# GLA stage of a hybrid layer on one core: from whole-sequence passes in fp32 to eight units of head pair and quarter with split fp32r products

## What is computed

```
gq, gk, gv, glr, gg = split(h @ w_in[:, :GLA_IN])         # 256, 256, 512, 16, 512 columns
log_a = log_sigmoid(glr @ gla_gate_up + gla_gate_bias) / 16
q = gq * 64**-0.5                                         # 4 heads, dk 64, dv 128
# chunks of 64 tokens, b = cumsum(log_a) within a chunk
q_in, k_in, k_st = q * exp(b), k * exp(-b), k * exp(b_last - b)
scores = tril(q_in @ k_in.T);  o_intra = scores @ v
S = S * exp(b_last) + k_st.T @ v                          # chunk after chunk
o = o_intra + q_in @ S_prev
gla_out = o * rsqrt(mean(o*o) + 1e-6) * gla_norm_w * silu(gg)
```

## Time and profile before

| | us |
|---|---|
| median of 3 runs | 3938.05 (3936.14 to 3941.47) |
| the profiled execution, its own time | 3943.03 |
| its span in the profile | 3941.3 |
| mean granted TensorE clock, share of full speed | 0.954 |
| TensorE busy in the span | 3507.1 |
| VectorE, ScalarE, GpSimd busy | 1894.0, 1273.3, 798.4 |

### The profile page before, as it was taken

One profiled execution on the slowest core, in us unless ns is written; L12 is line 12 of the kernel. 1 busy time (PEld: TensorE's weight loads), 2 busy tenths in 40 slices (PEclk: granted clock), 3 DMA queues, 4 the chain that ended last, 5 costly groups with the idle time before them and its releaser, 6 DMA issues. The chain is left out here.

```text
span 3941.3 us, 72212 instructions
## 1 busy us (share of the span) xinstructions
PE 3507.1 (89%) x30237; PEld 2860.4 (73%) x30237; DVE 1894.0 (48%) x2915; ACT 1273.3 (32%) x1970; POOL 798.4 (20%) x592
## 2 busy tenths in 40 slices
PE   6989989899698898797999998960699999999998
PEld 4777878778534344586888886850699999999997
DVE  4455656556522133366212225669455555555553
ACT  3343534444221222233000002330344444444442
POOL 3333434333167093000000000011010010110100
PEclk9999999999899899898999999985899999999999
DMA  4121121111132131343110105440466666666663
GB/s 129 45 79 45 43 82 43 55 47 29 60 121 79 44 107 33 128 136 94 27 53 27 53 11 183 155 138 13 158 199 218 203 214 204 201 218 207 208 207 86
DMA packets 357752, 431.44 MB, mean 109 GB/s; under 512 B 14788, under 2 KB 301684, under 8 KB 356004
## 3 DMA queue, kind: packets, MB, share of 16 engines
q1 hardware_dynamic: 348328, 394.82, 31.1%
q0 software_dynamic: 9216, 33.56, 3.6%
HBM read 361.04 MB, written 67.13 MB: 109 GB/s over the span
## 5 line engine op out<-in xcount | busy, mean ns | idle before, releaser
L1983 PE MATMUL bank<-ex_x_hi,ex_w_lo 128*128 128x256 f32 x2048 | 580.3, 283 | 1.5 <-DVE ex_x_lo L2152 1.5
L1984 PE MATMUL bank<-ex_x_lo,ex_w_hi 128*128 128x256 f32 x2048 | 580.2, 283 | 0.0
L1985 PE MATMUL bank<-ex_x_hi,ex_w_hi 128*128 128x256 f32 x2048 | 580.1, 283 | 0.0
L1979 DVE TENSOR_TENSOR ex_w_lo<-ex_w_loaded,ex_w_hi 128x2048 fp32r<-128x2048 f32 x186 | 420.7, 2290 | 235.6 <-ACT ex_w_hi L1975 235.6
L1975 ACT ACTIVATE ex_w_hi<-ex_w_loaded 128x2048 fp32r<-128x2048 f32 x192 | 359.8, 1905 | 199.6 <-PE bank L1985 183.9
L1983 PEld LDWEIGHTS bank<-ex_x_hi,ex_w_lo 128*128 128x128 f32 x2048 | 393.9, 192 | 2.5 <-issue 1.9
L1984 PEld LDWEIGHTS bank<-ex_x_lo,ex_w_hi 128*128 128x128 f32 x2048 | 393.8, 192 | 0.6
L1985 PEld LDWEIGHTS bank<-ex_x_hi,ex_w_hi 128*128 128x128 f32 x2048 | 393.8, 192 | 0.0
L1227 PE MATMUL bank<-hidden_hT,gl_w_block 128*128 128x512 f32 x768 | 335.1, 599 | 1.4 <-ACT gl_ada_acc L1341 1.4
L1778 PE MATMUL bank<-sc_x_hi,sc_w_lo 128*128 128x512 f32 x768 | 300.4, 391 | 21.8 <-DVE sc_hT_lo L1814 16.3
L1779 PE MATMUL bank<-sc_hT_lo,sc_w_hi 128*128 128x512 f32 x768 | 299.5, 390 | 0.0
(11 more groups left out here) (334 smaller groups left out, 7083.6 us busy)
## 6 DMA issues: line engine op xcount, KB each, us to landing
ex_w_loaded<-in_wg SPq DMA_DIRECT2D x64, 1024.0 KB, 5.2
ex_w_loaded<-in_wu SPq DMA_DIRECT2D x64, 1024.0 KB, 6.5
ex_w_loaded<-in_wd SPq DMA_DIRECT2D x64, 1024.0 KB, 5.2
rw_w_loaded<-in_w_in SPq DMA_DIRECT2D x68, 512.0 KB, 3.9
gl_ada_tile<-in_ada_w SPq DMA_DIRECT2D x48, 512.0 KB, 3.9
sc_w_loaded<-in_sc_w_in SPq DMA_DIRECT2D x24, 512.0 KB, 6.9
rw_x_tile<-in_x SPq DMA_DIRECT2D x16, 512.0 KB, 4.9
hT_dram<-rw_h_staged SPq DMA_DIRECT2D x32, 256.0 KB, 2.8
```

The costliest lines, as they stand in the source:

```text
L1979: engine.tensor_tensor(w_lo[c % SPLIT][:], raw[:, c % LOADED, :], w_hi[c % SPLIT][:].bitcast(F32), ALU.subtract).then_inc(s["lo"], 1)
L1983: nc.tensor.matmul(psum, ll, rh, start=first, stop=False)
L1984: nc.tensor.matmul(psum, lh, rl, start=False, stop=False)
L1985: return nc.tensor.matmul(psum, lh, rh, start=False, stop=last)
```

## The change

The stage no longer holds h for the whole sequence. It works in eight units u = 4*gp + q, gp a pair of heads and q a quarter of 512 tokens, unrolled, with no barrier in between; `hT` is made after the stage.

- Products: each h quarter is loaded in two halves into one buffer `hs`, split by ScalarE in four pieces of 128 x 1024 (`split_h`) into `h_hi`, and by VectorE (`low_h`) into `h_lo`; one buffer each. The first two pieces of the next quarter may be written when g1 is half done (`h_free`), the others when it is done. The weights of a pair are split once (`split_w`, `low_w`) and stay for its four units. All products are three fp32r matmuls: gate rank (only for u < 4), k, q, g0, g1 with 512 columns; the values token-major (h is the stationary side) with 256 columns, so v needs no turn.
- Two PSUM banks take all jobs in turn (`begin` waits until the job two before has been read).
- Core of unit c = u - 1 among the products of unit u: four turns of k_st, eight score products, 16 state terms in four quadrants, o inside (channel-major: v as the stationary side), o of the state (64 rows, 64 columns, 16 of them), and the variance by a matmul with a matrix of 1/128. A state buffer of 16 chunks lets the eight updates of a unit run one after the other.
- rsqrt and silu come from Exp and Ln: factor = exp(-0.5*ln(var + eps) + log_sigmoid(g)) * g * norm weight; Silu and Sqrt are gone.
- ada: the loads go out six tiles per unit; the same two GpSimd instructions per tile; the six sums of a half in units 3 and 7.
- Stores of 128 x 512 per unit and head.

```diff
-def gla(nc, k, hT, w_in, gate_up, gate_bias_col, norm_col, mT, ada_w, ada_b):
+def gla(nc, k, w_in, gate_up, gate_bias_col, norm_col, mT, ada_w, ada_b):
...
+                def begin(key):
+                    n = len(job)
+                    job[key] = n
+                    before.append(key)
+                    if n >= 2:
+                        pe.wait_ge(*read_of(before[n - 2]))
+                    return bank[RB[n % 2]]
...
+                    for kb in range(KD):
+                        if first:
+                            h_ready(u, kb)
+                        nc.tensor.matmul(psum[0:rows, :], lo[:, kb, :], h_hi[:, kb, :], start=(kb == 0), stop=False)
+                        nc.tensor.matmul(psum[0:rows, :], hi[:, kb, :], h_lo[:, kb, :], start=False, stop=False)
+                        mm = nc.tensor.matmul(psum[0:rows, :], hi[:, kb, :], h_hi[:, kb, :], start=False, stop=(kb == KD - 1))
+                        if last and kb == KD // 2 - 1:
+                            mm.then_inc(s["h_free"], 1)
...
+                for u in range(NU):
+                    c = u - 1
+                    if u < Q:
+                        lr(u)
+                    values(u, 0)
+                    z(u)
+                    if c >= 0:
+                        turn_and_score(c)
+                    values(u, 1)
+                    if c >= 0:
+                        state_terms(c)
+                        o_inside(c)
+                    block_product(u, "k")
+                    if c >= 0:
+                        o_of_state(c)
+                    block_product(u, "q")
+                    if c >= 0:
+                        variance(c)
+                    if u == Q - 1:
+                        ada_sums(u)
+                    block_product(u, "g0")
+                    block_product(u, "g1", True)
+                c = NU - 1
+                turn_and_score(c)
+                state_terms(c)
+                o_inside(c)
+                ada_sums(c)
+                o_of_state(c)
+                variance(c)
...
+                for u in range(NU):
+                    if u + 1 < NU:
+                        load_h(u + 1, 0)
+                        load_h(u + 1, 1)
+                    if u == Q - 1:
+                        load_w(NB)
+                        load_w(NB + 1)
...
+                    for m in range(6 * u, 6 * u + 6):
+                        ada(m)
...
+                    if u:
+                        store(u - 1)
...
+                def keep_gate(u, h):
+                    n = 2 * u + h
+                    psum = psum_of(f"g{h}", u)
+                    act.wait_ge(s["job"], job[(f"g{h}", u)] + 1)
+                    if u:
+                        act.wait_ge(s["mult"], n - 1)
+                    nc.scalar.activation(gn[h][:], psum, ACT.Copy, scale=nw[:, 0:1]).then_inc(s["g_copied"], 1)
+                    nc.scalar.activation(lsg[h][:], psum, ACT.Abs).then_inc(s["g_abs"], 1)
+                    act.wait_ge(s["g_abs"], n + 1)
+                    nc.scalar.activation(lsg[h][:], lsg[h][:], ACT.Exp, scale=-1.0).then_inc(s["g_exp"], 1)
+                    act.wait_ge(s["g_exp"], n + 1)
+                    nc.scalar.activation(lsg[h][:], lsg[h][:], ACT.Ln, bias=1.0).then_inc(s["g_ln"], 1)
...
+                    keep_values(u, 0)
+                    gate(u)
...
+                    if c >= 0:
+                        keep_turned(c)
...
+                    exponents(u)
...
+                    if c >= 0:
+                        square_o(c)
...
+                    if u == Q - 1:
+                        keep_ada(u)
+                    if c >= 0:
+                        log_of_variance(c)
+                        factor(c)
+                    if u == Q - 1:
+                        split_w(NB + 3)
+                    keep_gate(u, 0)
+                    if u + 1 < NU:
+                        for p in range(4):
+                            split_h(u + 1, p)
+                    keep_gate(u, 1)
...
+                    if c >= 0:
+                        combine(c)
...
+                    log_sigmoid(u, 0)
+                    if u + 1 < NU:
+                        for p in range(4):
+                            low_h(u + 1, p)
+                    log_sigmoid(u, 1)
```

More of the change, by code:

```diff
@@ L1147, in gla @@
+        vt = sb(nc, ctx, "v_tokens", [P, 2, 4, 2 * P])
+        ktok = sb(nc, ctx, "k_tokens", [P, 4, P])
+        scm = sb(nc, ctx, "scores", [P, 2, 4, P])
+        S = sb(nc, ctx, "state", [P, 16, P])
+        gn, lsg, osq, fac, ob = [[sb(nc, ctx, f"{n}{h}", [P, QT]) for h in range(2)] for n in ("gate", "log_sigmoid", "o_square", "factor", "out")]
+        mean = sb(nc, ctx, "mean", [P, P])
+        eps = sb(nc, ctx, "eps", [P, 1])
         ada_t = sb(nc, ctx, "ada_tile", [P, 2, ADA_W])
         ada_acc = sb(nc, ctx, "ada_acc", [P, 3 * D])
-        ada_in = (s["ada_w0"], s["ada_w1"])
+        bank = k.bank
@@ L1150, in gla @@
+        heads2 = [slice(0, 64), slice(64, 128)]
+        quads = [(0, 0), (1, 1), (0, 1), (1, 0)]
+        RB = (0, 1)
         NA = 3 * KD
[L1151 to L1156, removed]
-        with nc.Block() as block:
+        blocks = ("v0", "v1", "k", "q", "g0", "g1")
@@ L1159, in _, with load_h @@
             @block.sync
             def _(sp):
-                sp.dma_start(wl[:], wv[:, :, GLA_LR:GLA_LR + RANK]).then_inc(s["wl"], 16)
[L1162 to L1174, removed]
+                def load_h(u, half):
+                    q = u % Q
+                    if u:
+                        sp.wait_ge(s["h_lo"], 4 * u - 2 + 2 * half)
+                    sp.dma_start(hs[:, 4 * half:4 * half + 4, :], k.hT_dram[4 * half:4 * half + 4, :, q * QT:(q + 1) * QT].rearrange("k p t -> p k t")).then_inc(h_in[half], 16)
@@ L1176, in _ @@
+                ada_last(1)
+                store(NU - 1)
+                sp.wait_ge(s["ada_stored"], 32)
+                for h in range(2):
+                    sp.wait_ge(stored[h], 16 * NU)
             @block.scalar
             def _(act):
[L1178 to L1181, removed]
-        meet(nc, s)
@@ new lines, in log_of_variance, with factor @@
+                def log_of_variance(c):
+                    for h in range(2):
+                        act.wait_ge(s["var"], 2 * c + h + 1)
+                        wait_for(act, s["out"], 2 * (c - 1) + h + 1)
+                        nc.scalar.activation(fac[h][:], bank[2 + h][:], ACT.Ln, bias=eps[:, 0:1]).then_inc(s["lnv"], 1)
+                def factor(c):
+                    for h in range(2):
+                        act.wait_ge(s["comb"], 2 * c + h + 1)
+                        nc.scalar.activation(fac[h][:], fac[h][:], ACT.Exp).then_inc(s["f"], 1)
@@ new lines, in keep_ada @@
+                def keep_ada(u):
+                    for n in range(6):
+                        act.wait_ge(s["job"], job[("ada", u, n)] + 1)
+                        nc.scalar.activation(ada_acc[0:1, n * 512:(n + 1) * 512], psum_of("ada", u, n)[0:1, :], ACT.Copy).then_inc(s["ada_row"], 1)
+                act.wait_ge(s["wl"], 16)
+                nc.scalar.activation(wl_hi[:], wl[:], ACT.Copy).then_inc(s["wl_hi"], 1)
+                for p in range(4):
+                    split_h(0, p)
+                split_w(0)
```

584 lines of the change are left out of this document (346 added, 238 removed).

## The result

The kernel after takes 3834.15 us in the median of four runs (3833.87 to 3834.46), the kernel before 3937.1 beside it (3934.55 to 3941.47): a ratio of 0.9737, 95% interval 0.9723 to 0.9752. The forecast was 3834. In the profiled execution (3834.46 us) the span is 3832.2, 109.1 under that of the profiled execution of before; between the medians the difference is 103.0.

The account below looks back on a forecast made before the run. TensorE was taken to bound the GLA stage (busy 488 of 554 us). Products, core, waits, head and tail summed to 443.9 us against 553.3, 109.4 less than the profiled 3943.0: 3834 us, range 3803 to 3876.

Parts of the forecast that it names:

- k of unit 0: Start of the stage: the first k product waits 1.9 us for its weights behind gate(0).
- tail: From the end of the last unit's g1 to the next stage's first load: 30.4 us.
- Products and core: TensorE work: split fp32r products and z take 295.1 us; seven cores among products at 9.2 each take 64.4.
- All this costs nothing: Within a unit, gate, turned keys and states finish before TensorE needs them, covered by v1, k and q.
- The boundaries: Between units TensorE waits for h's split and the gate: seven boundaries, 23.6 us.
- low_h falls when GpSimd is idle, save at the first boundaries: 2 us: VectorE's low parts of h meet GpSimd's ada work only at the first boundaries, costing 2 us.
- Rival (1): Boundary longer: low parts of h beside GpSimd take 2.45 us each, 23 us more, 3857; 3871 if combine slows; chance 0.24.
- The wait for GpSimd: In unit 3 the six ada sums wait 5.6 us for GpSimd's last tiles; tile 18 lands about 5 us in.
- The head: Stage start: 3.1 MB load ahead of the parameters TensorE needs, 11.5 us to first matmul, then 3 of low clock.
- Rival (2), no changes of table: Exp and Ln share one set, so 64 loads vanish, with 23 us at boundaries and 6 in the tail: 3805; chance 0.12.
- Rival (3), the clock: Boundary gaps drop TensorE to 1.2 GHz, doubling affected products and core; at half, +190 us, 4024; chance 0.05.
- Rival (4): Part of the change does nothing: GpSimd's sums already existed, so they bring 0, counted as 0; no separate chance.

Follow-up runs that it names:

- the serial kernel: Changed kernel with the whole core of unit u-1 ahead of unit u's products instead of among them; stage 480.0 us (+32.4), run 3867.61 us.
- the kernel with Tanh: Changed kernel with silu(g) from Tanh instead of Exp and Ln, the variance factor adapted; stage 432.1 us (-15.5), run 3822.75 us.
- the kernel with the tiles moved: Changed kernel with ada tiles dealt 7, 7, 7, 3 over the first four units instead of six each; stage 435.2 us (-12.4), run 3825.81 us.
- the last variant: Changed kernel with tiles, Tanh, tail and head edits, plus z ahead of the values in units 4 to 7; stage 419.0 us, run 3807.18 us.
- the best kernel: Changed kernel with tiles 7, 7, 7, 3, Tanh gate, last unit's scores before g1, parameters issued earlier, k's split before the values' copy; stage 416.4 us, run 3806.79 us.
- its repetition: The changed kernel run once more, unaltered, on the same chip; stage 447.2 us, run 3832.93 us.

## Why the prediction was right

The mechanism and the stage's length were right, within 4 us in 444; that 3834 met 3834.15 is luck. The sum was taken from the one profiled execution at 3943.0, 5 us above the median of before. From that median, 3938.05, the same 109.4 would have given 3828.7, and the medians differ by 103.0.

Against the stage, term by term (forecast, then after):

| term | forecast | after |
|---|---|---|
| first load to first matmul | 11.5 | 13.6 |
| low clock at the start | 3 | 2.4 |
| products and core, unit 6 | 43.3 | 43.2 |
| k of unit 0 | 1.9 | 1.8 |
| boundaries, keep_ada, GpSimd beside low_h | 23.6 + 0.9 + 2 | 23.3 |
| wait for GpSimd in unit 3 | 5.6 | 10.3 |
| the sums behind it | 5.5 | 7.9 |
| tail | 30.4 | 29.4 |

The differences add up to +4.2, and the stage was 3.7 longer than forecast.

*Products and core* were the large terms, and held: starts 0.227 and 0.120 apart. In the core the scores cost less (1.10 for eight, not 1.7: the 0.42 for two in the earlier trace rows held what a group costs at its two ends, once and not per product) and z more (1.05, not 0.86). "All this costs nothing" held for the whole chain of the core, and the serial kernel prices the cover, net of the boundary waits that it hides: 32 us.

*The boundaries* came out 3.2 under the forecast, with two errors against each other. Without GpSimd they cost 17.3, not 23.6. The pieces of h were split 0.95 us apart, not 1.06, and in the later units nothing waited behind the values for z. But "low_h falls when GpSimd is idle, save at the first boundaries: 2 us" was wrong. The tiles of a unit ran past its end, and it cost 6. Rival (1) named this mechanism, at 23 us if every low part took 2.45: it is real, at a quarter of that price. The 1.20 us of the earlier trace rows were read as a slower rate, and were a wait: 15 of those 16 began 0.62 us into a GpSimd instruction of 1.27 us (L1072) and ended 0.55 us after it. In the same way a low part here pays only when it meets GpSimd at the wrong moment (median 1218 ns, seven of 32 longer, the worst 3418). The Trainium skill (SBUF — State Buffer, "Who interferes with whom") says that two SBUF inputs on VectorE contend with a reading GpSimd, and calls what they share an exclusive lock. For GpSimd's additions the trace agrees (the last section has the numbers); beside its scaling (L1680) the low part at 1122.34 began 1.18 us into one and still took 1226 ns, so not all of that instruction blocks.

*The wait for GpSimd* was read in the right place and 4.7 us too short. Tile 18 was scaled from 1241.48, 8 us into the unit instead of 5, since SP issues it behind h and two weight blocks; and the six tiles took 5.8 each, not 5.5, also because GpSimd waits in turn (one scaling, at 1252.53, took 4.87 us instead of 2.84 while VectorE made the low parts of two weight blocks). The 2.4 on the sums were not forecast at all: low clock after that gap.

*The head* was 2.1 too short: the sum counted bytes (in proportion to the earlier trace rows they give 12.8; the 11.5 isn't worked out), and SP's issue of one small DMA took 3.48 us behind the weight blocks.

*Rival (2), no changes of table*, fell by its premise: 63 loads of 1283 ns stayed, though the stage now uses Exp and Ln with plain copies and squares alone. The Trainium skill (ScalarE: Activation LUTs, "Table sets: the hidden batching unit") has both in one set; this program's trace disagrees, as the earlier trace rows did. (It has tanh in a set with exp; there the trace agrees: the kernel with Tanh has no load between the two, and 33 loads in all.) Its price was wrong too, 29 us against 13 measured, because keep_gate lies only partly on the path, as the boundary also waits for the pieces of h, and six loads ran during a wait.

*Rival (3), the clock:* there is low clock behind gaps, in all some 9 us (2.4 at the start, 2.3 at two boundaries, 2.7 at the sums, 1.6 in the tail), and the stage kept 0.95. It never became a state of the stage. *Rival (4)*: GpSimd's sums brought nothing, as said; their new deal costs 13 in unit 3, of which dealing them 7, 7, 7, 3 gives 12.4 back.

## What to carry to other kernels

Put a serial chain in pieces between products that last longer than its links, and price the cover by taking it away once. A step dealt evenly over the units is not free because its sum fits: what counts is the last piece ahead of its reader. And where a stage's gain is smaller than the scatter of the stages beside it, cut the stage out of the trace and judge that.

## What the runs showed of the hardware

- **The clock falls after some short gaps, and not after others as long.** Starts nearly twice as far apart follow gaps of 10.3, 6.1 and 4.1 us, one of 2.75 in the kernel with the tiles moved, and three of 2.16 in the last variant (one is above); but not that variant's gap of 2.17 at 1274.38, nor one of 2.28 in the best kernel (at 1322.82). TensorE's timeline of the kernel with the tiles moved, and the window behind it:

```profile
1228.22 0.39 PE L1217 MATMUL bank<-gl_h_hi,gl_w_lr_lo 128*16 128x512 f32 x1 [2.75 <-DVE gl_h_lo L1567]
1228.44 0.43 PE L1218 MATMUL bank<-gl_h_lo,gl_w_lr_hi 128*16 128x512 f32 x1
1228.68 0.62 PE L1219 MATMUL bank<-gl_h_hi,gl_w_lr_hi 128*16 128x512 f32 x1
1229.10 0.63 PE L1217 MATMUL bank<-gl_h_hi,gl_w_lr_lo 128*16 128x512 f32 x1
```

```profile
1229.00:1232.00 3.00, 3.00 (x8) 1.00 (x7) 3.00 (x3) 2.96 (x4) 2.92 (x2) 0.50 1.02 268
```

  The starts go from 0.22 to 0.42 apart two matmuls after the gap, and the granted clock is 0.50 there: the lower of the two levels, 1.2 GHz. Where the clock falls it costs, beside the gap itself, 1.6 us behind the gaps of 2.75, 4.1 and 6.1, 1.6 to 2.5 behind those of 2.16 and 2.7 behind that of 10.3: it is not in proportion to the gap. What decides whether it falls stays open.
- **Products on half of the rows overlap in full.** The eight scores of two heads on different rows (16 records, 1400.48 to 1401.58) start in pairs 0.006 apart, and the pairs follow 0.11 apart, which is what one record of the same 128 columns on all rows takes (inside of o, 16 records from 1408.56 to 1410.37). The pair of before in the earlier trace rows does the same.
- **A VectorE instruction with two inputs in SBUF waited for the end of a GpSimd addition under way.** In after, in its repetition and in the kernel with the tiles moved, 16 such instructions (13 low parts, 3 scans) began while an addition (L1683) was under way, and all of them ended 1.08 or 1.09 us after it, however long it still had to run (0.22 to 2.34 us): alone they take 1.22. It goes both ways: GpSimd's scaling takes up to 4.88 us beside a row of low parts, and 2.84 at its fastest.
- **The bracket understates.** A modelled matmul lasts longer than the distance of regular starts (0.39 against 0.227, 0.28 against 0.120), so each stall shows some 0.16 us less than it costs.
